# First MLP product: blocks 2 to 15 as seven half-size products, with the weight sums and the gate row moved

## The chip, the cores and the metric

The kernel runs on one core of one Trainium2 chip. The metric is device time in microseconds of one launch; lower is better. Each launch computes one layer for 512 frames of width 2048.

## The reference, cut to what matters

The change touches the second sub-layer and the adaLN gate of that sub-layer:

```python
mod = (c_act @ w_ada[i] + b_ada[i])          # six parts of 2048; the last is gate_f
h = rmsnorm(x, g_pre_mlp[i]) * (1.0 + scale_f) + shift_f       # (512, 2048)
y = jnp.square(jax.nn.relu(h @ w_mlp_in[i])) @ w_mlp_out[i]    # hidden width 8192
x = x + gate_f * rmsnorm(y, g_post_mlp[i])
```

"First MLP product" is h @ w_mlp_in, followed by the squared relu. Everything is float32.

## The kernel before

Every float32 operand of a matmul is split in two: a rounded high part (written by ScalarE, type float32r) and the low part, which is the operand less the high part (written by VectorE). A product is then three matmuls, high x high, high x low, low x high. `split_mm` (lines 847 to 851) issues them; lines 849, 850 and 851 are the three lines that the profile shows for TensorE.

The first MLP product runs over 16 blocks of 512 hidden features (FBS = 16). `mlp_in(b)` (line 1221) goes over 16 k-tiles and four tiles of 128 features, each `split_mm` with the weights as the stationary operand and 512 frames moving: 192 matmuls of 512 columns a block. Blocks alternate between two sets of four PSUM banks. Block 0 (`first_mlp_in`) is cut in pieces that follow the arrival of x.

Weights come in groups of four k-tiles, four groups (`MM_O`) a block, 1 MB each: SP's queue loads them (`load_m1`), ScalarE makes the high part (`split_hi_mlp`), VectorE the low part (`split_lo_mlp`), in two buffers. Each engine has its own program order, written out by hand, and semaphores couple them.

Behind a block, `hidden(b - 1)` runs on ScalarE (relu, square, high parts) and on VectorE, where four operations form the combinations (lines 2458 to 2464) that the second MLP product needs, since that product already works by seven half-size products for a pair of quarters; line 2469 makes their low parts. The finished hidden block (14 rows of 512 numbers a partition, 3.6 MB) goes to DRAM in two stores of 1.8 MB each (`store_hidden`), for blocks 0 to 13. Two hidden buffers alternate.

The gate row gate_f = c_act @ w_ada + b_ada is made in eight parts of 256 columns between the blocks: ScalarE scales one half of a loaded tile by c_act and GpSimd the other (`ada_times_c`, `ada_second`), VectorE sums over k (`ada_reduce`, line 1892), TensorE sums over partitions with a matrix of ones (`ada_rows`), VectorE adds the bias and multiplies by the gain (`gate_row`). GpSimd does nothing else in this stage. In the second MLP product it adds operands for the quarter sums (`b22_sums`, line 2764).

## Time and profile before

| | |
|---|---|
| time, median of 3 runs | 2184.85 us (2184.24 to 2184.99) |
| span of the profiled execution | 2183.1 us |
| TensorE busy | 2152.5 us, 99% of the span |
| VectorE, ScalarE, GpSimd busy | 1542.9, 892.7 and 356.4 us (71%, 41%, 16%) |
| DMA | 445.46 MB, mean 204 GB/s |

The page has no time of the profiled execution other than its span. The busy share of an engine is counted from its instructions; a matmul's record is longer than the distance to the next, so that distances between starts tell the rate. The first MLP product lies between about 871 and 1557 us, the second behind it.

### The profile page before, as it was taken

How to read it: one execution, taken by the hardware profiler on the slowest of the kernel's cores; microseconds unless marked ns; L12 is line 12 of the kernel's file. 1: busy time of each engine (PE TensorE's matmuls, PEld its weight loads, DVE VectorE, ACT ScalarE, POOL GpSimd, SP SyncE). 2: the span in 40 equal slices, each digit the busy share in tenths (PEclk: the TensorE clock that was granted, in tenths of full speed). 3: DMA queues.
4: the chain of work that ended last, by engine and by line, in shares of the span. 5: the costliest groups of instructions: out<-in, count | busy, mean ns of one | idle time of the engine just before them, and what ended most of it. 6: DMA issues, size and time to landing. Idle time of an engine off the chain costs nothing.

```text
span 2183.1 us, 26860 instructions
## 1 busy us (share of the span) xinstructions
PE 2152.5 (99%) x9807; PEld 1753.1 (80%) x9807; DVE 1542.9 (71%) x1618; ACT 892.7 (41%) x1197; POOL 356.4 (16%) x206
## 2 busy tenths in 40 slices
PE   6999999999999999999999999999999999999998
PEld 4688888777777888888888888888888888888886
DVE  7987667677887626744554365445789898898988
ACT  5353433342343325543533443435444444444443
POOL 1000000000000001000000000000036454453634
PEclk9999999999999999999999999999999999999999
DMA  9967657655554343665574665655374666567764
GB/s 361 355 223 229 211 159 249 199 174 167 152 149 154 135 174 141 221 207 189 207 249 164 207 233 206 207 190 181 117 269 147 238 214 200 172 241 238 246 219 167
DMA packets 259333, 445.46 MB, mean 204 GB/s; under 512 B 18380, under 2 KB 102672, under 8 KB 253592
## 3 DMA queue, kind: packets, MB, share of 16 engines
q1 hardware_dynamic: 258976, 443.91, 60.5%
q8 instruction: 71, 1.16, 0.2%
q14 instruction: 38, 0.31, 0.0%
q10 hardware_dynamic: 248, 0.08, 0.0%
HBM read 384.14 MB, written 59.79 MB: 203 GB/s over the span
## 4 chain that ended last, share of the span: by engine, by line
PE 93%; DVE 2%; DMA 1%; SPq 1%; ACT 1%; issue 1%; DVEq 1%; POOL 0%; POOLq 0%; ACTq 0%
PE pair L849 29%; PE pair L851 29%; PE pair L850 29%; DMA am_item<-in_w_ada 1%; PE pair L1068 1%; PE pair L952 1%; PE pair L926 1%; SPq L667 0%; PE pair L943 0%; DMA w_raw<-in_w_in 0%; PE pair L992 0%; PE pair L1146 0%; PE pair L1041 0%; DVE gg L1927 0%; DVE w_lo L1835 0%
## 5 line engine op out<-in xcount | busy, mean ns | idle before, releaser
L849 PE MATMUL pair<-in_hi,w_hi 128*128 128x512 f32 (+1 forms) x1728 | 689.0, 399 | 0.1
L851 PE MATMUL pair<-in_hi,w_lo 128*128 128x512 f32 (+1 forms) x1728 | 670.8, 388 | 0.0
L850 PE MATMUL pair<-in_lo,w_hi 128*128 128x512 f32 (+1 forms) x1728 | 669.8, 388 | 0.0
L849 PEld LDWEIGHTS pair<-in_hi,w_hi 128*128 128x128 f32 x1728 | 324.7, 188 | 69.5 <-issue 5.8
L851 PEld LDWEIGHTS pair<-in_hi,w_lo 128*128 128x128 f32 x1728 | 324.4, 188 | 68.4
L850 PEld LDWEIGHTS pair<-in_lo,w_hi 128*128 128x128 f32 x1728 | 325.0, 188 | 64.9 <-issue 1.9
L849 PE MATMUL pair<-v_op,hid_r 128*128 128x512 f32 x896 | 348.7, 389 | 0.3 <-issue 0.3
L851 PE MATMUL pair<-v_op,hid_r 128*128 128x512 f32 x896 | 348.6, 389 | 0.0
L850 PE MATMUL pair<-v_op,hid_r 128*128 128x512 f32 x896 | 348.6, 389 | 0.0
L1843 DVE TENSOR_TENSOR w_lo<-w_raw,w_hi 128x2048 fp32r<-128x2048 f32 x62 | 144.6, 2332 | 287.8 <-ACT w_hi L1324 287.8
L2499 DVE TENSOR_TENSOR v_op<-v_raw,v_op 128x1024 fp32r<-128x1024 f32 x192 | 295.5, 1560 | 64.8 <-ACT v_op L1802 63.7
L1802 ACT ACTIVATE v_op<-v_raw 128x1024 fp32r<-128x1024 f32 x192 | 203.3, 1061 | 286.2 <-PE pair L851 268.0
L1324 ACT ACTIVATE w_hi<-w_raw 128x2048 fp32r<-128x2048 f32 x63 | 120.5, 1913 | 234.2 <-PE pair L851 234.2
L2764 POOL TENSOR_TENSOR v_sum<-v_raw,v_raw 128x512 f32<-128x512 f32 x60 | 149.2, 2514 | 367.8 <-DVE v_raw L2514 367.8
L1835 DVE TENSOR_TENSOR w_lo<-w_raw,w_hi 128x1536 fp32r<-128x1536 f32 (+2 forms) x78 | 137.1, 1758 | 88.5 <-ACT w_hi L1315 88.0
L849 PEld LDWEIGHTS pair<-v_op,hid_r 128*128 128x128 f32 x896 | 168.2, 188 | 35.7 <-ACT v_op L1802 0.7
L851 PEld LDWEIGHTS pair<-v_op,hid_r 128*128 128x128 f32 x896 | 168.2, 188 | 35.0
L850 PEld LDWEIGHTS pair<-v_op,hid_r 128*128 128x128 f32 x896 | 168.2, 188 | 34.9
L1315 ACT ACTIVATE w_hi<-w_raw 128x1536 fp32r<-128x1536 f32 (+2 forms) x78 | 116.0, 1487 | 177.2 <-PE pair L851 165.2
L2773 POOL TENSOR_TENSOR v_raw<-v_raw,v_sum 128x512 f32<-128x512 f32 x60 | 135.3, 2286 | 18.4 <-DVE v_op L2499 18.4
L2685 POOL TENSOR_TENSOR ada<-ada,c_act 128x2048 f32<-128x2048 f32 x8 | 30.5, 3817 | 588.7 <-DMA ada<-in_w_ada 553.3
L2555 DVE TENSOR_TENSOR y_t<-pair,y_t 128x1024 f32<-128x1024 f32 x104 | 124.9, 1214 | 0.7 <-PE pair L851 0.7
(286 smaller groups left out, 2302.6 us busy)
## 6 DMA issues: line engine op xcount, KB each, us to landing
w_raw<-in_w_mlp_in SPq DMA_DIRECT2D x64, 1024.0 KB, 5.3
v_raw<-in_w_mlp_out SPq DMA_DIRECT2D x128, 512.0 KB, 5.1
hid_r<-hid_scratch SPq DMA_DIRECT2D x112, 512.0 KB, 6.4
hid_scratch<-hid_r SPq DMA_DIRECT2D x28, 1792.0 KB, 6.9
am_item<-in_w_ada SPq DMA_DIRECT2D x64, 512.0 KB, 8.3
...
```

What stands on the lines that cost most here:

```text
L849: pe.matmul(dst, a[0], b[0], start=start, stop=False, skip_group_check=onto)
L850: pe.matmul(dst, a[0], b[1], start=False, stop=False, skip_group_check=onto)
L851: return pe.matmul(dst, a[1], b[0], start=False, stop=stop, skip_group_check=onto)
L1315: act.activation(view(w_hi[n]), view(w_raw[n]), ACT.Copy).then_inc(hi_done, 1)
L1324: act.activation(m1_hi[m1_slot(j)][:, :], w_raw[j % 2][:, :], ACT.Copy).then_inc(hi_done, 1)
L1802: act.activation(v_op[i % 4][:, 0, :], raw_of(u, p)[:, h, :], ACT.Copy).then_inc(v_hi, 1)
L1835: dve.tensor_tensor(view(w_lo[n]), view(w_raw[n]), view(w_hi[n]).bitcast(F32), ALU.subtract)\
L1843: dve.tensor_tensor(m1_lo[m1_slot(j)][:, :], w_raw[j % 2][:, :], m1_hi[m1_slot(j)][:, :].bitcast(F32), ALU.subtract).then_inc(lo_done, 1)
L2499: dve.tensor_tensor(v_op[i % 4][:, 1, :], raw_of(u, p)[:, h, :], v_op[i % 4][:, 0, :].bitcast(F32), ALU.subtract).then_inc(v_lo, 1)
L2555: return dve.tensor_tensor(dst, src[:, :, :], dst, ALU.add)
L2764: last = pool.tensor_tensor(v_sum[:, h, cols], v_raw[q[B22]][:, h, cols], v_raw[q[B11]][:, h, cols], ALU.add)
L2773: last = pool.tensor_tensor(b21, b21, v_sum[:, h, cols], ALU.subtract)
```

## The change

Blocks 0 and 1 stay as they are. Each of blocks 2 to 15 is done in two half-blocks (`u` = 0 to 27; an even `u` is the first of its block). For the frames in two halves, the input features in two halves, and two groups of 128 hidden features of the block, the product is a 2 x 2 block product, and Winograd's form of Strassen's method makes it of seven products of half the size, in the order P1, P7, P6, P2, P5, P4, P3. Each is 8 `split_mm` with 256 columns. The sums of x that it needs (three tiles made new, one in place of a quarter of x) are made once, during block 1, by GpSimd and VectorE. The sums of weights are made for each half-block: the first, A21 + A22, on GpSimd (`sum_1`), three more on VectorE. Sums of results are made in PSUM: by accumulating onto a bank, by two copies on ScalarE, and by two additions on VectorE (`make_u3`, `make_c22`).

Weights come as quarters, 8 k-tiles x 128 columns, 512 KB in rows of 512 bytes, into five buffers; operands go through three buffers, one product each. There is one hidden buffer for blocks 0 to 14 in place of two, and relu and squares take 1024 elements at once. The gate row is made by 32 fused multiply-adds of 1024 columns on VectorE (`gf_step`) from whole rows of w_ada, with four sums over partitions on TensorE (`gf_rows`) and one multiplication by the gain each. The eight-part form of it, with its GpSimd and ScalarE work, is gone. Operand buffers of the second MLP product and the order of its PSUM pairs are renamed, and the last block's relus and squares go by quarters.

The diff, cut to its core:

```diff
-    M_END = M_MLP + FBS * MM_O
+    NB = 2
+    M_END = M_MLP + NB * MM_O
+    STEPS = 7
+    SUBS = 2 * (FBS - NB)
+    ALL_STEPS = STEPS * SUBS
...
+        A11, A21, A22, SUM, A12 = range(5)
+        SW_SLOT = ((0, 1, 2, 3, 4), (1, 0, 3, 2, 4))
+        SW_OPERAND = (A11, A21, A11, A12, SUM, A22, A12)
+        F_P1, F_P7, F_P6, F_P2, F_P5, F_P4, F_P3 = range(7)
+        C_X, C_Y, C_W, C_Z = range(4)
...
+            def load_quarter(u, role):
+                n = SW_SLOT[u % 2][role]
+                k = slice(0, XQ) if role in (A11, A21) else slice(XQ, KT)
+                col = block_of(u) * FBLK + (HALF if role in (A21, A22) else 0) + u % 2 * P
+                sp.dma_start(sw_raw[n][:, :, :], w_m1_t[:, k, col:col + P]).then_inc(sw_in[n], 16)
...
+            for u in range(SUBS):
+                b, following = block_of(u), u + 1 < SUBS
+                stored = u % 2 and b - 1 < FBS - 2
+                sp.wait_ge(sw_lo_done, step_end(u, F_P7))
+                if following:
+                    load_quarter(u + 1, A11)
+                else:
+                    sp.wait_ge(sw_used, step_end(u, F_P7))
+                    load_m2(0, B11)
+                    load_m2(0, B22)
+                if stored:
+                    store_hidden(b - 1, 0)
+                if following:
+                    sp.wait_ge(sw_lo_done, step_end(u, F_P6))
+                    sp.wait_ge(sw_sum, SW_SUM_0 + sums_of(u, S_4))
+                    load_quarter(u + 1, A21)
+                if stored:
+                    store_hidden(b - 1, 1)
+                if following:
+                    sp.wait_ge(sw_lo_done, step_end(u, F_P5))
+                    load_quarter(u + 1, A22)
+                    for g in GF_AT[u + 1]:
+                        load_gf(g)
+                    if u - 1 in GF_PART and GF_PART[u - 1] < 3:
+                        load_g_post(GF_PART[u - 1] + 1)
+                    sp.wait_ge(sw_lo_done, step_end(u, F_P3))
+                    load_quarter(u + 1, A12)
...
+            def strassen_in(u):
+                b, m = block_of(u), u % 2
+                for i in range(STEPS):
+                    n = STEPS * u + i
+                    pe.wait_ge(sw_hi_done, n + 1)
+                    pe.wait_ge(sw_lo_done, n + 1)
...
+                    if i == F_P7 and u - 1 in GF_PART:
+                        pe.wait_ge(gf_col, GF_COL_0 + GF_PART[u - 1] + 1)
+                    if i == F_P6:
+                        pe.wait_ge(p1_copied, u + 1)
+                    if i == F_P5:
+                        pe.wait_ge(u3_ready, u + 1)
+                    if i == F_P4 and u in GF_PART:
+                        gf_rows(u)
+                    if i == F_P3:
+                        pe.wait_ge(c22_ready, u + 1)
+                    dst = sub_bank(u, {F_P1: C_X, F_P2: C_X, F_P7: C_Z, F_P4: C_W}.get(i, C_Y))
+                    fresh = i in (F_P1, F_P7) and m == 0 or i == F_P7 and u == SUBS - 1
+                    for k in range(XQ):
+                        last = split_mm(dst, (sw_hi[n % 3][:, k, :], sw_lo[n % 3][:, k, :]), x_operand(i, k),
+                                        fresh and k == 0, k == XQ - 1, onto=True)
+                    last.then_inc(sw_used, 1)
...
+            def split_hi_step(n):
+                u, i = divmod(n, STEPS)
+                if i in (F_P1, F_P2, F_P4):
+                    done, count = sw_arrived(u, SW_OPERAND[i])
+                    act.wait_ge(done, count)
+                else:
+                    act.wait_ge(sw_sum, SW_SUM_0 + sums_of(u, {F_P7: S_3, F_P6: S_2, F_P5: S_1, F_P3: S_4}[i]))
...
+                else:
+                    act.wait_ge(sw_used, n - 2)
+                act.activation(sw_hi[n % 3][:, :, :], sw_tile(u, SW_OPERAND[i])[:, :, :], ACT.Copy).then_inc(sw_hi_done, 1)
...
+                for i in range(STEPS):
+                    if i == F_P2:
+                        copy_p1(u)
+                    if i == F_P5:
+                        copy_p7(u)
+                    split_hi_step(STEPS * u + i)
...
+                    if m == 0 and i in (F_P6, F_P2):
+                        relus(b - 1, i - F_P6)
+                    if m == 0 and i in (F_P5, F_P4):
+                        squares(b - 1, i - F_P5)
+                    if m == 0 and i == F_P3:
+                        hidden_hi(b - 1, 0)
+                    if m == 1 and i == F_P7:
+                        hidden_hi(b - 1, 1)
+                    if i == F_P6 and u in GF_PART:
+                        gf_high(GF_PART[u])
...
+            def x_sum(n):
+                dst, a, b, op = ((t1_raw, B12_HI, B11_HI, ALU.subtract), (t1_raw, t1_raw[:, :, :], t1_dif[:, :, :], ALU.add),
+                                 (t2_raw, B22_HI, t1_raw[:, :, :], ALU.subtract), (t2_raw, t2_raw[:, :, :], B22_LO, ALU.add),
+                                 (t4_raw, B21_HI, t2_raw[:, :, :], ALU.subtract), (t4_raw, t4_raw[:, :, :], B21_LO, ALU.add))[n]
+                if n == 0:
+                    dve.wait_ge(mod_lo, KT + N_PIECES)
+                    dve.wait_ge(x_tr, KT + N_PIECES)
+                if n == 1:
+                    dve.wait_ge(xs_pool, XS_POOL_0 + 4)
+                if n:
+                    dve.wait_ge(xs_raw, XS_RAW_0 + n)
+                dve.tensor_tensor(dst[:, :, :], a, b, op).then_inc(xs_raw, 1)
...
+            x_sum(0)
+            split_lo_mlp(MM_O)
+            x_sum(1)
+            x_sum(2)
+            split_lo_mlp(MM_O + 1)
+            combine(0, slice(0, SEQ), squares_to(0)).then_inc(h_comb, 1)
+            hidden_lo(0, 0)
+            x_sum(3)
+            split_lo_mlp(MM_O + 2)
+            hidden_lo(0, 1)
+            x_sum(4)
+            x_sum(5)
+            split_lo_mlp(MM_O + 3)
+            dve.memset(gg[:, :], 0.0).then_inc(gf_zero, 1)
+            x_low(0)
+            x_low(1)
+            def sum_3(u):
+                done, count = sw_arrived(u, A11)
+                dve.wait_ge(done, count)
+                dve.wait_ge(sw_sum, SW_SUM_0 + sums_of(u, S_1))
+                dve.tensor_tensor(sw_tile(u, A21)[:, :, :], sw_tile(u, A11)[:, :, :], sw_tile(u, A21)[:, :, :], ALU.subtract)\
+                    .then_inc(sw_sum, 1)
+            def sum_2(u):
+                dve.wait_ge(sw_lo_done, step_end(u, F_P1))
+                dve.wait_ge(sw_sum, SW_SUM_0 + sums_of(u, S_3))
+                dve.tensor_tensor(sw_tile(u, A11)[:, :, :], sw_tile(u, SUM)[:, :, :], sw_tile(u, A11)[:, :, :], ALU.subtract)\
+                    .then_inc(sw_sum, 1)
+            def sum_4(u):
+                dve.wait_ge(sw_lo_done, step_end(u, F_P2))
+                dve.wait_ge(sw_sum, SW_SUM_0 + sums_of(u, S_2))
+                dve.tensor_tensor(sw_tile(u, A12)[:, :, :], sw_tile(u, A12)[:, :, :], sw_tile(u, A11)[:, :, :], ALU.subtract)\
+                    .then_inc(sw_sum, 1)
+            def split_lo_step(n):
+                u, i = divmod(n, STEPS)
+                dve.wait_ge(sw_hi_done, n + 1)
...
+                    dve.wait_ge(sw_used, n - 2)
+                dve.tensor_tensor(sw_lo[n % 3][:, :, :], sw_tile(u, SW_OPERAND[i])[:, :, :],
+                                  sw_hi[n % 3][:, :, :].bitcast(F32), ALU.subtract).then_inc(sw_lo_done, 1)
+            def make_u3(u):
+                dve.wait_ge(sw_used, step_end(u, F_P6))
+                dve.wait_ge(p7_copied, u + 1)
+                dve.wait_ge(h_relu, relus_to(block_of(u) - 2))
+                dve.tensor_tensor(sub_bank(u, C_W), sub_bank(u, C_Y), p7_sb[:, :], ALU.add).then_inc(u3_ready, 1)
+            def make_c22(u):
+                dve.wait_ge(sw_used, step_end(u, F_P5))
+                dve.tensor_tensor(sub_bank(u, C_Z), sub_bank(u, C_Y), p7_sb[:, :], ALU.add).then_inc(c22_ready, 1)
+            def gf_step(g):
+                half, k = divmod(g, GF_ITEMS)
+                dve.wait_ge(gf_in[g % 2], GF_IN_0 + 16 * (g // 2 + 1))
...
+                    dve.wait_ge(gf_used, g)
+                part = gg[:, 1024 * half:1024 * half + 1024]
+                dve.scalar_tensor_tensor(part, gf_item[g % 2][:, :], c_act[:, k:k + 1], part, ALU.mult, ALU.add)\
...
+            def strassen_in(u):
+                b, m = block_of(u), u % 2
+                n0 = STEPS * u
+                if u == 0:
+                    sum_3(0)
+                split_lo_step(n0 + F_P1)
+                sum_2(u)
+                for g in GF_AT[u][:1]:
+                    gf_step(g)
+                if m == 1:
+                    hidden_lo(b - 1, 0)
+                split_lo_step(n0 + F_P7)
+                split_lo_step(n0 + F_P6)
+                if u == 0:
+                    x_low(2)
+                if m == 1:
+                    hidden_lo(b - 1, 1)
+                split_lo_step(n0 + F_P2)
+                sum_4(u)
+                if u == 0:
+                    x_low(3)
+                for g in GF_AT[u][1:]:
+                    gf_step(g)
+                split_lo_step(n0 + F_P5)
+                make_u3(u)
+                if u in GF_PART:
+                    gf_low(GF_PART[u])
+                split_lo_step(n0 + F_P4)
...
+                if m == 0:
+                    combine(b - 1, slice(0, SEQ), squares_to(b - 1)).then_inc(h_comb, 1)
+                split_lo_step(n0 + F_P3)
+                if u + 1 < SUBS:
+                    sum_3(u + 1)
+                make_c22(u)
+                if u in GF_PART:
+                    gf_columns(u)
...
-            with pool.Fori(0, FBS // 2) as g:
-                ada_second(g + Q_GF)
-            pool.wait_ge(ada_col, Q_GF + FBS // 2)
+            pool.wait_ge(w_used, M_MLP + 1)
+            pool.wait_ge(x_tr, KT + N_PIECES)
+            left, right = slice(0, HALF), slice(HALF, SEQ)
+            b12_lo = in_lo[:, 0:XQ, right].bitcast(F32)
+            pool.tensor_tensor(t3_raw[:, :, :], in_hi[:, XQ:KT, right].bitcast(F32), in_hi[:, 0:XQ, right].bitcast(F32),
+                               ALU.subtract).then_inc(xs_pool, 1)
+            pool.tensor_tensor(t3_dif[:, :, :], in_lo[:, XQ:KT, right].bitcast(F32), b12_lo, ALU.subtract).then_inc(xs_pool, 1)
+            pool.wait_ge(xs_pool, XS_POOL_0 + 2)
+            pool.tensor_tensor(t3_raw[:, :, :], t3_raw[:, :, :], t3_dif[:, :, :], ALU.add).then_inc(xs_pool, 1)
+            pool.tensor_tensor(t1_dif[:, :, :], b12_lo, in_lo[:, 0:XQ, left].bitcast(F32), ALU.subtract).then_inc(xs_pool, 1)
+            def sum_1(u):
+                for role in (A21, A22):
+                    done, count = sw_arrived(u, role)
+                    pool.wait_ge(done, count)
+                if u:
+                    pool.wait_ge(sw_lo_done, step_end(u - 1, F_P4))
+                pool.tensor_tensor(sw_tile(u, SUM)[:, :, :], sw_tile(u, A21)[:, :, :], sw_tile(u, A22)[:, :, :], ALU.add)\
+                    .then_inc(sw_sum, 1)
+            for u in range(SUBS):
+                sum_1(u)
```

## Rows read from the trace of the kernel before

**Rows 1.** Page, part 4: the chain that ended last, by engine.

```profile
PE 93%; DVE 2%; DMA 1%; SPq 1%; ACT 1%; issue 1%; DVEq 1%; POOL 0%; POOLq 0%; ACTq 0%
```

**Rows 2.** Stretches, first MLP product: busy us per engine, clock, DMA share, GB/s.

```profile
871.00:1571.00 700.00, 699.87 (x3137) 580.74 (x3137) 367.73 (x237) 293.28 (x370) 30.54 (x8) 1.00 0.60 202
```

**Rows 3.** ScalarE timeline (start us, duration us): first relu of blocks 0 and 5.

```profile
901.17 2.64 ACT L1705 ACTIVATE hid_f<-pair 128x512 f32<-128x512 f32 x4 [2.88 <-PE pair L851]
...
1119.99 2.58 ACT L1705 ACTIVATE hid_f<-pair 128x512 f32<-128x512 f32 x4 [7.17 <-PE pair L851]
```

**Rows 4.** TensorE timeline: two 256-column matmuls, nine starts apart.

```profile
850.47 0.28 PE L851 MATMUL pair<-in_hi,m_lo 128*128 128x256 f32 x1
...
851.54 0.28 PE L851 MATMUL pair<-in_hi,m_lo 128*128 128x256 f32 x1
```

**Rows 5.** VectorE timeline: prices and pitches of the operations that come up.

```profile
17.51 0.75 DVE L2113 SCALAR_TENSOR_TENSOR am_acc<-am_item,c_act,am_acc 128x512 f32<-128x512 f32 x1
18.17 0.75 DVE L2113 SCALAR_TENSOR_TENSOR am_odd<-am_item,c_act,am_odd 128x512 f32<-128x512 f32 x1
...
910.71 1.76 DVE L2469 TENSOR_TENSOR hid_r<-hid_f,hid_r 128x1536 fp32r<-128x1536 f32 x1
...
1117.27 0.42 DVE L1950 TENSOR_TENSOR gg<-pair,bg_bc 128x256 f32<-128x256 f32 x1 [2.12 <-PE pair L907]
...
1126.61 0.68 DVE L2458 SCALAR_TENSOR_TENSOR hid_f<-hid_f 128x512 f32<-128x512 f32 x1
...
1707.09 1.23 DVE L2499 TENSOR_TENSOR v_op<-v_raw,v_op 128x1024 fp32r<-128x1024 f32 x1 [1.50 <-ACT v_op L1802]
1708.23 2.35 DVE L2555 TENSOR_TENSOR y_t<-pair,y_t 128x1024 f32<-128x1024 f32 x2
1710.50 2.28 DVE L2514 TENSOR_TENSOR v_raw<-v_raw,v_raw 128x2048 f32<-128x2048 f32 x1
```

**Rows 6.** Timeline of GpSimd beside VectorE: who waits for whom.

```profile
1129.12 3.79 POOL L2685 TENSOR_TENSOR ada<-ada,c_act 128x2048 f32<-128x2048 f32 x1 [84.27 <-DMA ada<-in_w_ada]
1129.46 7.25 DVE L2469 TENSOR_TENSOR hid_r<-hid_f,hid_r 128x1536 fp32r<-128x1536 f32 x2
...
1712.91 2.15 POOL L2764 TENSOR_TENSOR v_sum<-v_raw,v_raw 128x512 f32<-128x512 f32 x1 [17.88 <-DVE v_raw L2514]
1713.83 2.32 DVE L2499 TENSOR_TENSOR v_op<-v_raw,v_op 128x1024 fp32r<-128x1024 f32 x1
```

**Rows 7.** Timeline of ScalarE: rounding a 1024-element operand.

```profile
1700.56 1.06 ACT L1802 ACTIVATE v_op<-v_raw 128x1024 fp32r<-128x1024 f32 x1 [1.66 <-PE pair L851]
```

**Rows 8.** DMA view: issues, KB each, median us to landing.

```profile
hid_scratch<-hid_r SPq DMA_DIRECT2D x28, 1792.0 KB, 6.9
ada<-in_w_ada SPq DMA_DIRECT2D x16, 1024.0 KB, 10.4
```

**Rows 9.** Timeline of SP's queue: issue of two loads with rows of 512 bytes.

```profile
1115.63 4.95 SPq L627 DMA_DIRECT2D ada<-in_w_ada  x2
```

**Rows 10.** Stretches: a load with 512-byte rows, and a hidden store, in transfer.

```profile
1123.00:1124.00 1.00, 1.00 (x6) 0.84 (x5) 0.00 (x0) 1.00 (x1) 0.00 (x0) 1.00 1.20 295
1139.00:1140.00 1.00, 1.00 (x6) 0.84 (x5) 0.00 (x0) 0.00 (x0) 0.00 (x0) 1.00 1.09 459
```

**Rows 11.** Timelines of GpSimd and VectorE at the end of block 0.

```profile
897.44 3.62 POOL L2685 TENSOR_TENSOR ada<-ada,c_act 128x2048 f32<-128x2048 f32 x1 [35.39 <-DVE in_lo L2376]
898.32 4.88 DVE L1843 TENSOR_TENSOR w_lo<-w_raw,w_hi 128x2048 fp32r<-128x2048 f32 x1 [1.12 <-ACT w_hi L1324]
```

**Rows 12.** TensorE's last group; stretches behind it (clock stands before DMA share).

```profile
2174.15 1.02 PE L1306 MATMUL pair<-y_t,v_sum 128*128 128x512 f32 x2
...
2175.00:2180.00 5.00, 0.17 (x1) 0.00 (x0) 4.33 (x5) 0.60 (x1) 0.00 (x0) 0.87 0.96 366
2180.00:2183.00 3.00, 0.00 (x0) 0.00 (x0) 0.00 (x0) 0.00 (x0) 0.00 (x0) 0.50 0.67 258
```

More of the change, by code:

```diff
@@ L272, in build_block @@
         w_in_s = [sem("w_in0"), sem("w_in1")]
-        ada_in = [sem(f"ada_in{u}") for u in range(2)]
         am_in = [sem(f"am_in{s}") for s in range(4)]
@@ new lines, in _ @@
+            store_hidden(0, 1)
+            sp.wait_ge(hi_done, M_END - 1)
+            sp.wait_ge(lo_done, M_END - 1)
+            load_quarter(0, A11)
+            load_quarter(0, A21)
+            sp.wait_ge(hi_done, M_END)
+            sp.wait_ge(lo_done, M_END)
+            load_quarter(0, A22)
+            sp.wait_ge(gf_zero, GF_ZERO_0 + 1)
+            sp.dma_start(gg[0:1, :], b_ada[0:1, GATE_F:GATE_F + D]).then_inc(gf_row, 16)
+            load_g_post(0)
+            sp.wait_ge(w_used, M_END)
@@ new lines, in hidden_hi @@
+            def hidden_hi(b, part):
+                hb = 1 if b == LAST else 0
+                act.wait_ge(h_sq, squares_to(b))
+                if part:
+                    act.wait_ge(h_comb, b + 1)
+                a, z = ((0, 3), (3, 7))[part]
+                act.activation(hid_r[hb][:, a:z, :], hid_f[hb][:, 7 + a:7 + z, :], ACT.Copy).then_inc(h_hi, 1)
+            for mm in range(MM_O):
+                if mm == 1:
+                    continue
+                split_hi_mlp(MM_O + mm)
+                if mm == 0:
+                    relus(0, 0)
+                    relus(0, 1)
+                    split_hi_mlp(MM_O + 1)
+                    squares(0, 0)
+                    squares(0, 1)
+                    hidden_hi(0, 0)
+                    hidden_hi(0, 1)
@@ new lines, in last_relu, with last_relu_one @@
+            def last_relu(first, half, done, count):
+                act.wait_ge(done, count)
+                cols = slice(half * HALF, half * HALF + HALF)
+                act.activation(hid_f[1][:, 6 + first:8 + first, cols], pair[2 * ((LAST + half) % 2) + first // 2][:, :, cols], ACT.Relu)\
+                    .then_inc(h_relu, 1)
+            def last_relu_one(n, done, count):
+                act.wait_ge(done, count)
+                act.activation(hid_f[1][:, 6 + n, RIGHT], bank[4 * (1 - LAST % 2) + n][:, RIGHT], ACT.Relu).then_inc(h_relu, 1)
@@ L1739, in raw_ready @@
+            for u in range(SUBS):
+                strassen_in(u)
             def raw_ready(u, p, h):
@@ L2479, in _ @@
[L2479 to L2493 removed]
+                    dve.wait_ge(sw_used, ALL_STEPS - 1)
@@ L2495, in split_operand, with hidden_end @@
+            for u in range(SUBS):
+                strassen_in(u)
+            def hidden_end():
+                combine(LAST, HIGH, squares_to(LAST)).then_inc(h_comb, 1)
+                hidden_lo(LAST, 0)
+                split_operand(3)
+                split_operand(4)
+                hidden_lo(LAST, 1)
+                split_operand(5)
+                seam_b12(0)
+                seam_sum(0)
             def split_operand(i):
```

469 lines of the change are left out of this document (282 added, 187 removed).

## The prediction

> **What bounds the kernel now.** I read the page first. TensorE is the chain: 93% of what ended last is its own work [rows 1], so time is gained only by fewer TensorE microseconds, and lost wherever TensorE is made to wait. Then the stretch view of the first MLP product: TensorE is busy 699.9 of 700 us, VectorE only 367.7 (53%), ScalarE 293.3, GpSimd 30.5, DMA engines 60% [rows 2]. The other engines have slack there on average; the change spends it. The relus of block 0 and of block 5 start 218.82 us apart, so a block takes 43.76 us [rows 3], 192 matmuls of 512 columns and a few small ones.
>
> **The gain.** A half-block (128 of the block's hidden features in each of the two halves, over all frames) becomes seven products of 8 x 3 matmuls of 256 columns. Nine starts of such matmuls with a weight load each lie 1.07 us apart, 0.119 us each [rows 4]. So a product is 24 x 0.119 = 2.85 us, a half-block 19.97, a block 39.95 against 43.76. Over 14 blocks that is -53.3 us if TensorE never waits. What remains is to see whether it waits. It does, at four places.
>
> **Prices.** VectorE, by pitch of successive operations [rows 5]: 1024 elements 1.15 us (1707.09 to 1708.23), 2048 elements 2.2, fused multiply-add with a column 0.66 for 512, so some 1.2 for 1024; 1536 elements 1.7; 256 elements from PSUM 0.42; the four combination steps of a hidden block 2.85 (1126.61 to 1129.46 in rows 6). ScalarE rounds 1024 elements in 1.06 [rows 7].
>
> GpSimd against VectorE is the price that matters. While GpSimd's 3.79 us operation ran, two VectorE operations worth 3.9 took 7.25: VectorE stood nearly as long as GpSimd worked. In the pair below, the VectorE operation that came while GpSimd had its turn took 2.32 for 1.2, and GpSimd's 512 elements took 2.15, of which the first 0.9 were a wait for VectorE's previous operation [rows 6]. They take turns by whole instructions when both read two operands in SBUF; GpSimd's own share is 1.1 us per 512 elements. So 1024 elements hold VectorE 2.2 us, 2048 hold it 4.4. The bounds are 0 (GpSimd's turn falls where VectorE waits anyway) and 2.2 per half-block; I take the full one where VectorE is late.
>
> The Trainium skill (GPSIMD Engine Reference, Engine selection) says that an elementwise sum of a tile belongs on VectorE and is about twice as slow on GpSimd. By it the first weight sum would cost VectorE 1.15 instead of 2.2; the rows' hold agrees in size, so here the move takes nothing off VectorE.
>
> **VectorE over one block.** 14 low parts and 6 sums x 1.15 = 23.0, four small ones 1.7, combination 2.85, low parts of the hidden block 3.9, 2.3 gate steps x 1.2 = 2.7, GpSimd's hold 2 x 2.2 = 4.4: 38.5 of 39.95 us. It was about 23. Nothing is left for its waits, and it waits in order: for P6 before `make_u3`, for the next half-block's GpSimd sum before `sum_3`, and `make_c22`, on which TensorE's last product P3 waits, stands behind `sum_3`.
>
> **First half of a block** (u even; zero is TensorE's start of P1; products end at 2.85, 5.7, 8.55, ...). P6 done 8.55, high part of P4 9.6, low part 10.8, combination of the previous block 13.65, low part of P3 14.8, `sum_3` 15.95, `make_c22` 16.4; GpSimd's sum falls into this (its A22 is asked for at 8.4 and is there at about 12) and holds it 2.2: 18.6. TensorE wants P3 at 17.1. Stall 1.5, half-block 21.5.
>
> **Second half** (u odd). VectorE enters 2.85 before zero and has two operations, a gate step, the first hidden low part (1.7) and P7's low part before TensorE's second product: 1.15 + 1.15 + 1.2 + 1.7 + 1.15 = 6.35, ready at 3.5 where 2.85 is wanted: stall 0.65. Then P6 4.65, second hidden low part 6.85, P2 8.0, `sum_4` 9.15 (A21 is asked for), P5 10.3 (A22 is asked for). SP's order puts both stores of the previous hidden block into the same queue ahead of A22. A store is 1.84 MB at 459 GB/s, 4.0 us; a quarter is 0.52 MB, 1.75 us at 295 [rows 10]. Issuing 2048 rows costs SP 2.5 us, a quarter's 1024 rows about 1.2 [rows 9]. A store lands 6.9 us after issue, of which 4.0 are transfer [rows 8]; I give a quarter 0.8 ahead and 0.9 behind. A11 is asked for at 3.5 and moves to 6.1; first store to 10.3; A21 12.1; second store 16.2; A22 18.1, landed 19.0. GpSimd's sum 21.2, `sum_3` 22.35, `make_c22` 22.8, against 17.8 wanted: stall 5.0. The half-block ends at 25.65. The bounds of this stall: 0.4 if A22 overtakes the store (landed 13.75, then VectorE's order alone: low part of P3 14.4, hold 16.6, `sum_3` 17.75, `make_c22` 18.2), 6 if the stores move at half the rate.
>
> A block is 21.5 + 25.65 = 47.15, with 0.1 for each of three restarts 47.45: +3.7 over 43.76. Blocks 2 to 14 have a store in their second half: 13 x 3.7 = +48. Block 15 has none, and no successor's sum: 21.5 + 20.6 = 42.1, -1.7.
>
> **The entrance** (block 1, where the sums of x are made). GpSimd and VectorE are released together at 897.4, behind the last low part of x [rows 11]. VectorE's first x difference 897.3 to 899.5; GpSimd's first of four 2048-element operations to 903.9; only then the low part of block 1's first weight group, 906.1. It ended at 903.2 before, just in time: stall 2.9. The next in VectorE's order, `x_sum(1)`, waits for all four of GpSimd: 910.5, 914.9, 919.3; two x sums 923.7, then the second group's low part 926.1. TensorE wants it at 906.2 + 10.9 = 917.1: stall 9.0. Later groups come in time. Together +12 (bounds 6 and 16: GpSimd's price per 2048 between the 3.6 of its broadcast multiply and 5). In the first half-block the low parts of x and the late loads of A22 and A12 put `make_c22` some 3.5 later than in the others: +3.5.
>
> **The rest.** The gate row loses 8 pairs of 256-column matmuls (8 x 0.24 = 1.9, contained in the 43.76 of a block) and has four pairs of 512 columns, 8 x 0.227 = +1.8. Its 32 multiply-adds are in VectorE's sum; eight 3.8 us GpSimd multiplies, sixteen VectorE reductions and ScalarE's scaling go, all of it hidden before, worth nothing. Loads of w_ada stay about the size they were and follow A22. ScalarE has per block 14 x 1.06 and 8 or so for the hidden block and copies, 23 of 40: hidden. The seam to the second product: last relus and squares by quarters on ScalarE, +1 (0 to 4). Renamed PSUM pairs and moved operand buffers cost nothing: the same number of banks, no order changed.
>
> **Sum**, on the profiled execution (span 2183.1): -53.3 is contained in the blocks; +48 - 1.7 + 12 + 3.5 + 1.8 + 1 = +64.6, a span of 2247.7. The page gives no time around the span; the median of the runs lies 1.75 above it, so 2249.5, rounded 2250.
>
> **Rivals.**
> 1. *The covers hold: faster.* GpSimd's turn falls into VectorE's waits, the stores don't delay A22, and TensorE runs through: -53.3 + 12 + 1.8 + 1 = -38.5, 2146. For it: VectorE was busy 53% [rows 2]. Against it: the sum of 38.5 in 39.95. It decides as soon as `make_c22` ends by 17.1 in both halves.
> 2. *The stores alone don't obstruct* (A22's packets slip in between). Second half 21.0, block 42.8, -1.0 x 13, with the entrance and the rest +4: 2189, between 2175 and 2205.
> 3. *The clock falls in the stalls.* Behind the last matmul group (ends about 2175.2) the granted clock is 0.87 on average over 2175 to 2180 and 0.50 after [rows 12]: full until about 2178.7, then 1.2 GHz. So idling 3.5 us brought it down once. A 5 us stall could; P3 at 1.2 GHz would take up to 24 x 0.107 = 2.6 more. 14 stalls x 0 to 2.6, say 2.3: +32, 2282. Against it: one observation, at the end of the program. The Trainium skill (TensorE: Matmul & The Clock Gate, HAM oscillation) describes this loss for a kernel that waits for a load between groups of matmuls.
> 4. *The change doesn't thin the columns' cost*: if a 256-column matmul cost 0.13 because three weight loads no longer hide, a block would be 43.7 without any stall. Rows 4 show 0.119 with the loads; the chance is small and it lies inside the slow cases.
>
> **Chances.** Forecast (2225 to 2268) 0.50; clock 0.18; stores out of the way 0.17, of which 0.09 slower, 0.04 the same, 0.04 faster; covers hold 0.15. Faster by over 0.2% (about what a measurement of this kernel can tell from no change) 0.19, within 0.2% 0.04, slower 0.77. The range goes from 2187 (into the second rival) to 2292 (the clock's full price); about 2 in 10 lie outside, nearly all on the fast side.
>
> **What would show it.** In the profile after: 256-column matmuls 0.119 apart within a product; TensorE idle ahead of P3, some 1.5 us in even and 5 in odd half-blocks, released by VectorE's `make_c22` addition; ahead of that `sum_3` waiting for GpSimd, and GpSimd for A22's DMA, whose landing takes 8 us or more in odd half-blocks and under 5 in even ones; VectorE over 80% busy in this stage; a stall of some 9 us at the second weight group of block 1; clock rows below 1.00 if rival 3 holds. If GpSimd's sum is done before VectorE reaches `sum_3`, or A22 lands early in the odd halves, the forecast is wrong on the side of the first two rivals.

## The result, and the profile after

The changed kernel takes 2320.74 us (median, 2318.82 to 2322.03) against 2184.76 for the kernel before: ratio 1.062, 95% interval [1.061, 1.064]. It is slower by 136 us, where +65 (2250, range 2187 to 2292) was forecast: the direction was right, the size half of what it is. The profiled spans are 2319.4 and 2183.1, 136.3 apart.

The page of the kernel after: busy times, the chain by engine, the two dearest groups of the new product, GpSimd's sum, and two kinds of DMA (last column: us from issue to landing).

```profile
PE 2156.3 (93%) x11815; PEld 1853.5 (80%) x11815; DVE 1745.4 (75%) x1903; ACT 968.7 (42%) x1222; POOL 423.0 (18%) x230
...
PE 68%; DMA 9%; DVE 9%; issue 6%; POOL 4%; ACT 2%; DVEq 1%; SPq 1%; POOLq 0%; ACTq 0%
...
L975 PE MATMUL pair<-in_hi,sw_hi 128*128 128x256 f32 x896 | 273.8, 306 | 117.7 <-DVE pair L2800 117.1
...
L3141 POOL TENSOR_TENSOR sw_raw<-sw_raw,sw_raw 128x1024 f32<-128x1024 f32 x28 | 74.6, 2663 | 672.0 <-DMA sw_raw<-in_w_mlp_in 672.0
...
sw_raw<-in_w_mlp_in SPq DMA_DIRECT2D x112, 512.0 KB, 4.9
...
hid_scratch<-hid_r SPq DMA_DIRECT2D x28, 1792.0 KB, 9.8
```

TensorE's own work was 93% of the chain [rows 1] and is 68% now. DMA, VectorE and GpSimd together are 22% of it, and the group of matmuls behind `make_c22` (L2800) stood 117.1 us. A hidden store lands 9.8 us after issue instead of 6.9 [rows 8].

The stretch view of the new product (busy us of TensorE, its weight loads, VectorE, ScalarE, GpSimd; then granted clock, DMA share, GB/s), beside [rows 2]:

```profile
1050.00:1500.00 450.00, 370.54 (x2862) 366.56 (x2862) 297.79 (x280) 194.86 (x207) 44.35 (x17) 0.91 0.53 179
```

TensorE is busy 82% instead of 100%, VectorE 66% though it is what TensorE waits for, and the clock is 0.91 on average. An engine busy for two thirds of a stage can hold the whole stage up if it waits in order. The waits of VectorE and GpSimd name whom it waits for (us in total, times, longest):

```profile
DVE sw_raw L2767 <- POOL sw_raw L3141: 142.9, 25, 9.9
...
DVE sw_lo L2789 <- ACT sw_hi L1928: 87.3, 69, 5.0
```

The first row is the stall's last link but one: `sum_3` waits for GpSimd's sum.

One odd half-block, followed back from the matmul that waited. First SP's queue, then GpSimd, VectorE and TensorE (start us, duration, in brackets the idle time before and its releaser):

```profile
1200.85 0.37 SPq L693 DMA_DIRECT2D sw_raw<-in_w_mlp_in  x1
1201.26 0.58 SPq L687 DMA_DIRECT2D hid_scratch<-hid_r  x1
1206.63 0.37 SPq L693 DMA_DIRECT2D sw_raw<-in_w_mlp_in  x1
1207.04 0.72 SPq L687 DMA_DIRECT2D hid_scratch<-hid_r  x1
1207.81 0.43 SPq L693 DMA_DIRECT2D sw_raw<-in_w_mlp_in  x1
1208.29 4.37 SPq L700 DMA_DIRECT2D gf_item<-in_w_ada  x1
```

```profile
1218.22 2.34 POOL L3141 TENSOR_TENSOR sw_raw<-sw_raw,sw_raw 128x1024 f32<-128x1024 f32 x1 [26.35 <-DMA sw_raw<-in_w_mlp_in]
```

```profile
1220.67 1.23 DVE L2767 TENSOR_TENSOR sw_raw<-sw_raw,sw_raw 128x1024 f32<-128x1024 f32 x1 [8.41 <-POOL sw_raw L3141]
1221.81 0.43 DVE L2800 TENSOR_TENSOR pair<-pair,p_sb 128x256 f32<-128x256 f32 x1
```

```profile
1222.38 0.55 PE L975 MATMUL pair<-in_hi,sw_hi 128*128 128x256 f32 x1 [6.79 <-DVE pair L2800]
1222.73 0.41 PE L976 MATMUL pair<-in_lo,sw_hi 128*128 128x256 f32 x1
1222.94 0.41 PE L977 MATMUL pair<-in_hi,sw_lo 128*128 128x256 f32 x1
...
1226.27 0.28 PE L977 MATMUL pair<-in_hi,sw_lo 128*128 128x256 f32 x1
1226.39 0.28 PE L975 MATMUL pair<-in_hi,sw_hi 128*128 128x256 f32 x1
```

A22, the quarter of weights that the sum waits for, is issued at 1207.81, behind two stores of 1.84 MB in the same queue. GpSimd gets to its sum at 1218.22, 10.4 us later, and passes it on at 1220.56. `sum_3` and `make_c22` follow, and TensorE has stood 6.79 us. `make_c22` itself reads neither A22 nor the sum; it only stands behind `sum_3`. When TensorE starts again its matmuls are 0.21 us apart, and 0.12 again from about 1225.7 on. The stretch view of that stall:

```profile
1219.00:1222.00 3.00, 0.00 (x0) 0.00 (x0) 1.33 (x2) 0.07 (x1) 1.56 (x1) 0.50 0.37 93
1222.00:1225.00 3.00, 2.62 (x12) 2.65 (x13) 2.97 (x4) 0.98 (x1) 0.00 (x0) 0.50 0.03 5
1225.00:1226.00 1.00, 1.00 (x8) 1.00 (x7) 1.00 (x2) 0.00 (x0) 0.00 (x0) 0.69 0.00 0
1226.00:1229.00 3.00, 3.00 (x27) 3.00 (x26) 1.85 (x2) 1.97 (x2) 0.00 (x0) 1.00 0.17 46
```

The granted clock is 0.50 (1.2 GHz) from 1219 on and stays there 3 us into the work. The Trainium skill (TensorE: Matmul & The Clock Gate, HAM oscillation) describes this loss: the clock falls while TensorE waits for a load, and the next products start slow. The rows agree with it.

**The 136 us by place.** The product starts at 962.2 instead of 946.9 (+15.3 in the entrance). Its 14 blocks end at 1693.1 instead of 1558.2, that is 730.9 us instead of 611.3 (+119.6). What follows is 1.4 longer. In the middle a block takes 52.63 us (twelve periods, from TensorE's restart at 1011.84 to that at 1643.38), where 47.45 was forecast. By the starts of the matmuls over these periods:

| us a block | forecast | measured |
|---|---|---|
| 336 matmuls and gate rows at full clock | 39.95 | 40.4 (0.1200 apart) |
| first matmuls after a pause | 0.3 | 0.3 |
| pauses between matmuls, pitch taken off | 7.15 | 9.45 |
| matmuls at the low clock, above their full-clock time | 0 | 2.4 |

The first row holds the gate row's matmuls too, which the forecast had in a term of its own (1.8 us over 14 blocks). The last row counts the intervals between 0.16 and 0.235 us, some 28 a block, less the 0.1 to 0.2 us a block which such intervals cost in the kernel that hardly waits (experiment `e11_p7_early` below).

### The profile page after: what moved, and what is told of

Same layout as the page of the kernel before. It is cut to its first block, busy times and chain, and to the rows that moved or that the text cites. A ratio compares the mean times of both kernels' runs of the same rounds, so it can differ in the third digit from the quotient of the medians.

```text
span 2319.4 us, 31846 instructions
## 1 busy us (share of the span) xinstructions
PE 2156.3 (93%) x11815; PEld 1853.5 (80%) x11815; DVE 1745.4 (75%) x1903; ACT 968.7 (42%) x1222; POOL 423.0 (18%) x230
## 4 chain that ended last, share of the span: by engine, by line
PE 68%; DMA 9%; DVE 9%; issue 6%; POOL 4%; ACT 2%; DVEq 1%; SPq 1%; POOLq 0%; ACTq 0%
PE pair L975 21%; PE pair L977 21%; PE pair L976 21%; DMA sw_raw<-in_w_mlp_in 9%; DVE sw_lo L2789 4%; POOL sw_raw L3141 3%; PE pair L1198 1%; PE pair L1082 1%; DVE gg L2810 1%; PE pair L1056 1%; DMA w_raw<-in_w_in 1%; DVE hid_r L2717 1%; ACT sw_hi L1928 1%; DVE sw_raw L2779 1%; PE pair L1073 0%
## 5 line engine op out<-in xcount | busy, mean ns | idle before, releaser
L975 PE MATMUL pair<-in_hi,sw_hi 128*128 128x256 f32 x896 | 273.8, 306 | 117.7 <-DVE pair L2800 117.1
L975 PE MATMUL pair<-in_hi,w_hi 128*128 128x512 f32 (+1 forms) x832 | 341.5, 410 | 12.5 <-DVE w_lo L2114 9.4
L1928 ACT ACTIVATE sw_hi<-sw_raw 128x1024 fp32r<-128x1024 f32 x196 | 207.5, 1059 | 343.1 <-PE pair L977 187.2
L977 PE MATMUL pair<-in_hi,w_lo 128*128 128x512 f32 (+1 forms) x832 | 323.1, 388 | 0.0
L976 PE MATMUL pair<-in_lo,w_hi 128*128 128x512 f32 (+1 forms) x832 | 322.1, 387 | 0.0
L2789 DVE TENSOR_TENSOR sw_lo<-sw_raw,sw_hi 128x1024 fp32r<-128x1024 f32 x196 | 244.9, 1255 | 88.2 <-ACT sw_hi L1928 87.3
L975 PEld LDWEIGHTS pair<-in_hi,sw_hi 128*128 128x128 f32 x896 | 189.8, 212 | 122.6 <-issue 121.8
L976 PE MATMUL pair<-in_lo,sw_hi 128*128 128x256 f32 x896 | 270.0, 301 | 0.0
L977 PE MATMUL pair<-in_hi,sw_lo 128*128 128x256 f32 x896 | 269.2, 300 | 0.0
L975 PEld LDWEIGHTS pair<-in_hi,w_hi 128*128 128x128 f32 x832 | 157.1, 189 | 47.9 <-issue 15.0
L975 PE MATMUL pair<-t_hi,sw_hi 128*128 128x256 f32 x672 | 190.6, 284 | 2.8 <-DVE sw_lo L2789 2.8
```

The costliest lines, as they stand in the source:

```text
L975: pe.matmul(dst, a[0], b[0], start=start, stop=False, skip_group_check=onto)
L976: pe.matmul(dst, a[0], b[1], start=False, stop=False, skip_group_check=onto)
L977: return pe.matmul(dst, a[1], b[0], start=False, stop=stop, skip_group_check=onto)
L1928: act.activation(sw_hi[n % 3][:, :, :], sw_tile(u, SW_OPERAND[i])[:, :, :], ACT.Copy).then_inc(sw_hi_done, 1)
L2789: dve.tensor_tensor(sw_lo[n % 3][:, :, :], sw_tile(u, SW_OPERAND[i])[:, :, :], sw_hi[n % 3][:, :, :].bitcast(F32), ALU.subtract).then_inc( ...
```

## The experiments

Ratios are to the kernel before (2184.7 to 2184.8 us). Theory: A22 lands late behind the stores; VectorE's fixed order hands that on to `make_c22` though it doesn't need it; every long stall also costs clock behind it. Rivals: VectorE or GpSimd is simply short of time; or the smaller matmuls are dear in themselves.

**`make_c22` ahead of `sum_3`** (`e1_c22_first`)

```diff
 split_lo_step(n0 + F_P3)
+make_c22(u)
 if u + 1 < SUBS:
     sum_3(u + 1)
-make_c22(u)
```

> Changed kernel with one edit: VectorE makes make_c22(u) before sum_3(u+1), so P3 no longer stands behind the chain A22 load, GpSimd sum, sum_3. Theory (order): the stall ahead of P3 goes in both halves (1.9 us in even, 6.9 in odd half-blocks of the trace after), but the low part of P1 of the next half-block still stands behind sum_3, one product (2.85 us) later, so the odd stall comes back there at about 4 us. Gain per block some 1.9 + 2.8 = 4.7 us, over 13 blocks some 60: about 2260. Rival (VectorE is simply full, 38.5 of 39.95 us counted): the stall only moves, total within 20 us of 2320.

Measured 2287.67 (2285.89 to 2290.40), ratio 1.047 [1.045, 1.049]: -33 where about -60 was expected. TensorE's waits:

```profile
PE pair L975 <- ACT sw_hi L1928: 64.5, 13, 6.3
PE pair L975 <- DVE sw_lo L2789: 25.5, 15, 2.2
```

The wait for `make_c22` is gone, but 13 waits of 5 us each (64.5 / 13) now stand at P1 of the next half-block. P1 needs no sum either: it reads A11, whose high part is long done, and its low part stands next behind `sum_3` on VectorE. The table names ScalarE's rounding, but the rounding that ends there is P7's, which waits for `sum_3`. The timeline of VectorE shows what P1 waited for: its low part ends at 1210.68, and TensorE starts at 1210.78:

```profile
1208.32 1.23 DVE L2767 TENSOR_TENSOR sw_raw<-sw_raw,sw_raw 128x1024 f32<-128x1024 f32 x1 [8.07 <-POOL sw_raw L3141]
1209.46 1.22 DVE L2789 TENSOR_TENSOR sw_lo<-sw_raw,sw_hi 128x1024 fp32r<-128x1024 f32 x1
```

So the late load is still there, and one reordering only moved the stall by a product.

**Stores behind A22** (`e2_stores_late`)

```diff
-if stored:
-    store_hidden(b - 1, 0)
 ...
-if stored:
-    store_hidden(b - 1, 1)
 if following:
     sp.wait_ge(sw_lo_done, step_end(u, F_P5))
     load_quarter(u + 1, A22)
+if stored:
+    store_hidden(b - 1, 0)
+    store_hidden(b - 1, 1)
```

> Changed kernel with one edit in SP's order: both stores of the hidden block are issued behind the load of A22 in place of ahead of it. Theory (queue): A22 lands some 5 us after its issue in odd half-blocks in place of 10.4, the stall there falls from 6.9 to some 1.5 us and the clock no longer drops there (it cost 1.4 us per stall): 13 x 6.5 = 85 us less, about 2235. Rival (latency of GpSimd and VectorE in the chain, not the queue): under 2 us a block, above 2295. What the delayed stores could cost: A12 and the gate rows land later; seen as a wait ahead of P2.

Measured 2258.49 (2256.91 to 2264.41), ratio 1.034 [1.033, 1.036]: -62 where 85 was expected.

```profile
PE pair L975 <- DVE pair L2800: 47.9, 27, 3.0
PE pair L975 <- DVE sw_lo L2789: 16.5, 19, 3.1
...
DVE gg L2810 <- DMA gf_item<-in_w_ada: 41.7, 12, 4.2
```

The wait for `make_c22` falls from 117.1 to 47.9; the stall in odd half-blocks is 1.9 us on average instead of 6.9. In exchange TensorE now waits 0.7 to 3.1 us ahead of P7 in most even half-blocks. The likely reason is that the gate rows' loads now lie behind the stores: VectorE waits 41.7 us for them in its order; this was not tested by itself. The experiment shows the queue: nothing but the place of two stores was changed. One stood ahead of A21 and both ahead of A22; now both stand behind these loads.

**The first weight sum on VectorE** (`e3_sum_on_vector`): the same addition, with the waits for its operands, at the head of `sum_3`; none on GpSimd.

```diff
-pool.tensor_tensor(sw_tile(u, SUM)[:, :, :], sw_tile(u, A21)[:, :, :], sw_tile(u, A22)[:, :, :], ALU.add)
+dve.tensor_tensor(sw_tile(u, SUM)[:, :, :], sw_tile(u, A21)[:, :, :], sw_tile(u, A22)[:, :, :], ALU.add)
```

> Changed kernel with the first of the four weight sums on VectorE (directly ahead of sum_3) in place of GpSimd. Theory (turns): GpSimd's 2.34 us is replaced by 1.15 in the chain ahead of P3 and holds VectorE no more: 1.2 us less per half-block, some 30 to 35 us in all, about 2288. Rival (VectorE is full and GpSimd relieves it): slower by 1.15 x 28 = up to 32 us, about 2350.

Measured 2292.75 (2289.83 to 2294.19), ratio 1.050 [1.048, 1.051]: -28, a little less than the 30 to 35 expected. TensorE's wait for `make_c22` is 90.1 us in 27 instead of 117.1.

**Another order in the entrance** (`e4_entrance`): both low parts of the first two weight groups ahead of the sums of x.

```diff
-x_sum(0)
 split_lo_mlp(MM_O)
-x_sum(1)
-x_sum(2)
 split_lo_mlp(MM_O + 1)
 combine(0, slice(0, SEQ), squares_to(0)).then_inc(h_comb, 1)
+x_sum(0)
 hidden_lo(0, 0)
 ...
```

> Changed kernel with VectorE's order in block 1 altered: the low parts of the first two weight groups come ahead of the sums of x. Theory: the stalls of 3.1 and 9.4 us at the first two weight groups go, and the low clock behind them (5 us off full in 900 to 950): 12 to 17 us less, about 2305. Rival (the sums of x then arrive too late for the first half-block): the stall moves behind block 1, less than 5 us gained.

Measured 2313.16 (2310.21 to 2320.33), ratio 1.060 [1.058, 1.062]: -7.6, where 12 to 17 was expected. Of the two entrance stalls (3.06 and 9.41) 1.0 and 4.5 are left, which the expectation took to go.

**Two orders together** (`e5_order_store`): `make_c22` and P1's low part ahead of `sum_3`, and the second store alone behind A22.

```diff
 if u == 0:
     sum_3(0)
-split_lo_step(n0 + F_P1)
+    split_lo_step(n0 + F_P1)
 ...
 split_lo_step(n0 + F_P3)
+make_c22(u)
 if u + 1 < SUBS:
+    split_lo_step(n0 + STEPS + F_P1)
     sum_3(u + 1)
-make_c22(u)
 ...
```

> Changed kernel with two edits: on VectorE make_c22(u) and then the low part of P1 of the next half-block ahead of sum_3(u+1); on SP the second store of the hidden block behind the load of A22 in place of ahead of it. Theory (order): with these, nothing that TensorE wants before P7 of the next half-block stands behind the load of A22 and GpSimd's sum, two products (5.7 us) more room than in the changed kernel; stalls of 9 us a block fall to under 1.5 and the clock stays up: a block about 41.5 us in place of 52.6, total about 2176. Rival (VectorE is full: 38.5 us of work counted in 39.95 us): a block stays at 44 us or more, above 2205, with TensorE waiting for low parts all over the half-block and not at one place.

Measured 2211.21 (2207.56 to 2213.96), ratio 1.013 [1.011, 1.014]: -109.5, against -145 expected. TensorE's wait for `make_c22` is 2.7 us, but it waits 26.2 us (16 times) for other low parts, all of them P7's, mostly 1.6 to 1.9 in odd half-blocks. The expectation took these as covered.

**With the entrance mended** (`e6_plus_entrance`): as the last, and in the entrance x sums 0 to 2 behind the third group's low part, the rest behind the fourth, and the low part of the second new x tile behind P1's.

> As e5_order_store, and VectorE's order in block 1 altered: low parts of the weight groups ahead of the sums of x, the low part of the second new x tile behind P1's. Theory: of the 3.1 and 9.4 us stalls some 3 to 5 us in all are left (low part of the third group, since GpSimd's four operations of 4.6 us hold VectorE in between): 8 to 12 us less than e5_order_store, about 2166. Rival: the sums of x arrive late for the first half-block, gain under 4.

Measured 2203.29 (2202.26 to 2204.02), ratio 1.008 [1.007, 1.010]: -7.9 by the edit, at the edge of what was expected.

**With the sum on VectorE** (`e7_plus_sum_on_vector`): as the last, with the edit of the third experiment.

> As e6_plus_entrance, with the first weight sum on VectorE in place of GpSimd. Theory (turns): GpSimd's 2.3 us hold is replaced by 1.15 us of VectorE's own work; where VectorE is close to the limit that is worth up to 1.15 us a half-block, 5 to 25 us less than e6. Rival (GpSimd's sum falls into VectorE's waits once the order is right): slower than e6 by up to 15.

Measured 2196.58 (2193.71 to 2199.25), ratio 1.005 [1.003, 1.007]: -6.7 by the edit, near the small end of what was expected.

**With the gate steps late** (`e8_plus_gate_late`): as the sixth, and the one or two gate steps of a half-block behind `make_u3`.

```diff
-for g in GF_AT[u][:1]:
-    gf_step(g)
 ...
-for g in GF_AT[u][1:]:
-    gf_step(g)
 split_lo_step(n0 + F_P5)
 make_u3(u)
+for g in GF_AT[u]:
+    gf_step(g)
```

> As e6_plus_entrance, with both gate multiply-adds of a half-block behind make_u3 in place of the first of them ahead of P7's low part. Theory: the 0.4 us wait ahead of P7 in odd half-blocks and any wait for the gate row's load go: 3 to 10 us less than e6. Rival: no change, as the multiply-adds only move to where make_c22 is due.

Measured 2184.15 (2182.35 to 2187.38), ratio 1.000 [0.999, 1.001]: -19 by the edit, two to six times what was expected. The first gate step stood ahead of P7's low part, for which the kernel of the fifth experiment waited.

**The clock by itself** (`e9_warm`): the changed kernel, and in its odd half-blocks TensorE multiplies a zero tile while it waits, which adds nothing to the result.

```diff
+zero_w = small("zero_w", [P, 32])
 ...
 if i == F_P3:
+    if m == 1 and u + 1 < SUBS:
+        for k in range(40):
+            pe.matmul(sub_bank(u, C_W)[0:32, :], zero_w[:, :].bitcast(F32R), t4_hi[:, k % XQ, :],
+                      start=False, stop=True, skip_group_check=True)
     pe.wait_ge(c22_ready, u + 1)
```

> The changed kernel with 40 matmuls of a zero weight tile (32 output columns, 256 moving ones, added onto a finished result, which they leave as it is) ahead of TensorE's wait for make_c22 in the 13 odd halves: TensorE works through about 4.8 us of the 6.9 us in which it stood. Theory: the idle stretch lets the clock fall, and in the changed kernel the matmuls behind the stall ran 0.213 us apart for 2.9 us (0.119 at the full clock), which costs 2.9 x (1 - 0.119/0.213) = 1.3 us a stall; without the fall 13 x 1.3 = 17 us go, to about 2304, and the granted clock of the stretch rises from 0.90 to 0.97 or more. Rival A: the clock costs more than that place shows (about 3 us a block are not accounted for by the stalls): about 2280. Rival B: the time behind the stall is set by VectorE's queue, which the clock does not touch, and a faster TensorE waits for it elsewhere: 2318 to 2321.

Measured 2302.29 (2298.12 to 2305.80), ratio 1.054 [1.052, 1.055]: -18.5 against -17 expected from the rows. No work was taken away; 520 matmuls came on top (13 x 40). It shows the clock's part, and not all of it:

```profile
1050.00:1500.00 450.00, 408.21 (x3276) 399.26 (x3276) 308.16 (x288) 200.52 (x212) 46.88 (x18) 0.97 0.53 181
...
1267.34 0.58 PE L976 MATMUL pair<-in_hi,sw_hi 128*128 128x256 f32 x1 [2.85 <-DVE pair L2805]
```

The clock is 0.97 instead of 0.91. It still falls where the zero products end before the wait does, as at 1267.34, where the first matmul behind 2.85 us of idleness takes 0.58 us instead of 0.36.

**Gate steps late, alone** (`e12_gate_late_alone`): the changed kernel with that one edit.

> The changed kernel with the one or two gate steps of a half behind make_u3, and nothing else. Theory: most gate steps stand ahead of weight steps with little slack, and in the kernel with the other orders mended this alone was worth 19 us; here the stalls at make_c22 are set by the landing of A22 and GpSimd's sum, so little of it is left: 2305 to 2318. Rival: the gate steps now stand nearer to sum_3 and make_c22 and push these later: 2322 to 2335.

Measured 2319.76 (2317.05 to 2321.21), ratio 1.062 [1.060, 1.063]: -1.0, which can't be told from nothing. The same edit was worth 19 us where the larger waits had gone.

**All of it** (`e10_sum_and_gate`) and **P7's low part early** (`e11_p7_early`): as the eighth with the sum on VectorE, then in addition:

```diff
+split_lo_step(n0 + F_P7)
 if m == 1:
     hidden_lo(b - 1, 0)
-split_lo_step(n0 + F_P7)
 split_lo_step(n0 + F_P6)
```

> All orders mended (make_c22 and P1's low part ahead of sum_3, the second store behind A22, the entrance, the gate steps behind make_u3) and the first weight sum on VectorE in place of GpSimd. Theory: the sum is no longer behind GpSimd's 2.34 us and its hand-over, worth 7 us in the kernel without the late gate steps; TensorE still waits 10.8 us for make_c22, of which half goes: about 2177 (2172 to 2182), below the kernel before. Rival: VectorE is busy 87% of the stretch already, and its 14 us more turn into waits for low parts: 2183 to 2192.

> As the kernel with the sum on VectorE and the gate steps late, and in addition P7's low part ahead of the first hidden low part in odd halves. Theory: TensorE's waits for a low part (10.2 us, 12 of them, in the kernel with the sum on GpSimd) are mostly those ahead of P7 in odd halves; they go, and the stores get their half a little later: 4 to 8 us less than the kernel without this edit, about 2170. Rival: the later hidden low part delays the first store and with it A21 and A22: the same or up to 5 us more.

Measured 2171.14 (2169.37 to 2172.64), ratio 0.994 [0.992, 0.995], and 2157.33 (2155.15 to 2158.44), ratio 0.987 [0.986, 0.989]: -13.0 by the sum (half of that was expected) and -13.8 by P7's low part (4 to 8 expected). TensorE's waits of the two in this product, and the stretch of the second:

```profile
PE pair L976 <- DVE sw_lo L2794: 13.1, 14, 1.7
...
PE pair L976 <- DVE sw_lo L2794: 1.3, 6, 0.5
...
1050.00:1500.00 450.00, 447.86 (x3707) 445.60 (x3707) 408.68 (x387) 251.39 (x269) 0.00 (x0) 1.00 0.67 226
```

The last kernel is the version that beats both: the change's arithmetic, with VectorE's and SP's orders made for it and one sum moved from GpSimd to VectorE, is 27.4 us (1.3%) faster than the kernel before. VectorE works 91% of the stretch, and TensorE hardly waits: it is busy 447.9 of 450 us. A block takes 41.0 us (1138.73 less 1015.62 is 123.1 for three).

## Why the prediction was wrong

*Right.* Each half-size matmul costs 0.120 with its weight load (forecast 0.119), so the fourth rival is out, and the gain is there: a block that hardly waits takes 41.0 us instead of 43.76. That is 2.8 a block where 3.8 was forecast (336 x 0.120 alone is 40.3; the gate row's matmuls and short pauses make up the rest). The place, the releaser and the order of the stalls were as forecast: in front of P3, long in odd and short in even half-blocks, released by `make_c22`, which stood behind `sum_3`, GpSimd and A22. The entrance was right to half a microsecond: stalls of 3.06 and 9.41 where 2.9 and 9.0 were forecast, because GpSimd's four operations ended at 904.28, 910.92, 915.59 and 920.10 where 903.9, 910.5, 914.9 and 919.3 were forecast. GpSimd's first two ran beside VectorE's operations and took 2.1 us longer than the last two, which ran alone:

```profile
897.58 6.70 POOL L3129 TENSOR_TENSOR t_raw<-in_hi 128x2048 f32<-128x2048 f32 x1 [35.22 <-DVE in_lo L2626]
904.24 6.68 POOL L3131 TENSOR_TENSOR t_dif<-in_lo 128x2048 f32<-128x2048 f32 x1
910.99 4.60 POOL L3133 TENSOR_TENSOR t_raw<-t_raw,t_dif 128x2048 f32<-128x2048 f32 x1
915.55 4.55 POOL L3134 TENSOR_TENSOR t_dif<-in_lo 128x2048 f32<-128x2048 f32 x1
...
899.75 6.68 DVE L2114 TENSOR_TENSOR w_lo<-w_raw,w_hi 128x2048 fp32r<-128x2048 f32 x1
920.13 2.29 DVE L2737 TENSOR_TENSOR t_raw<-t_raw,t_dif 128x2048 f32<-128x2048 f32 x1 [13.70 <-POOL t_dif L3134]
...
906.53 0.47 PE L975 MATMUL pair<-in_hi,w_hi 128*128 128x512 f32 x1 [3.06 <-ACT w_hi L1489]
927.10 0.77 PE L975 MATMUL pair<-in_hi,w_hi 128*128 128x512 f32 x1 [9.41 <-DVE w_lo L2114]
```

The first stall is put down to ScalarE, but VectorE's low part is what ends last there: 899.75 and 6.68 make 906.43.

*Wrong: the clock was left out of the sum.* The forecast took the stalls to leave the clock alone and gave the third rival, that it falls in them, 0.18. The rival was right: low-clock matmuls cost 2.4 us a block, 13 x 2.4 = 31, and about 2.2 more in the entrance, where eleven matmuls behind the 9.41 us stall were 0.43 apart instead of 0.23. That its price (+32) agrees with the sum is partly luck. It had 2.3 behind each long stall, with 0.107 for a matmul; the rows show 0.093 for a matmul and 1.9 behind each of the 13 long stalls, and the rest came behind shorter pauses, which it did not count. The zero products won 18.5 of it back by experiment. Of the 71.7 us that the forecast lacked, the clock made 33, the longer pauses 30 and the matmuls' own pace 6. The one row that spoke for it [rows 12], 3.5 us of idleness and then 0.50, was evidence enough for a 5 us stall; to call it one observation was the mistake. A shorter pause could do it as well, which that row had not shown. Behind one of 2.07 us the matmuls were 0.21 apart at once; behind the three of 1.50 they never were. Behind two of the seven pauses of 1.75 (up to 1299.24 and 1562.24) they started 0.12 apart and went over to 0.21 some 1.4 us later; the last two rows are the stretches of the first of these (TensorE's busy time, clock, DMA share, GB/s):

```profile
1194.58 0.36 PE L975 MATMUL pair<-in_hi,sw_hi 128*128 128x256 f32 x1 [1.50 <-DVE pair L2800]
1194.77 0.28 PE L976 MATMUL pair<-in_lo,sw_hi 128*128 128x256 f32 x1
...
1246.26 0.56 PE L975 MATMUL pair<-in_hi,sw_hi 128*128 128x256 f32 x1 [2.07 <-DVE pair L2800]
1246.61 0.42 PE L976 MATMUL pair<-in_lo,sw_hi 128*128 128x256 f32 x1
...
1299.00:1300.00 1.00, 0.76 (x6) 1.00 0.00 0
1301.00:1303.00 2.00, 2.00 (x11) 0.50 0.00 0
```

*Wrong in size: the odd stall.* Forecast 5.0, measured 6.9 (5.5 to 7.9 in the 13 of them). A22 was asked for 10.3 after the start of P1, as forecast, but the sum on GpSimd started 20.8 after it where 19.0 was forecast. The stores moved at about the rate used (444 GB/s for 459). It was the quarters that were priced too low. The sum had 295 GB/s for all of a quarter, but A11, issued at 1200.85, moved 74 and then 212 GB/s in its first two microseconds and its packets ran until about 1205, 7.5 after the start of P1 where 6.1 was forecast. A22 added some 0.4, and landed at 1218.10 (20.6 for 19.0). The end of `make_c22` came at 24.8 instead of 22.8. The stretches (TensorE's busy time, clock, DMA share, GB/s):

```profile
1202.00:1203.00 1.00, 1.00 (x11) 1.00 0.34 74
1203.00:1204.00 1.00, 1.00 (x10) 1.00 0.81 212
1204.00:1205.00 1.00, 1.00 (x11) 1.00 1.31 459
1206.00:1208.00 2.00, 2.00 (x19) 1.00 1.04 444
```

The forecast's mechanism is borne out by the store experiment. Its price for the stores in the odd half is 13 x (5.0 - 0.4) = 60 us; that run's -62 also holds clock won back and time lost to the late gate rows, so the agreement of the two figures is partly luck. SP's issue of a quarter took 0.37 us and not 1.2, which changed nothing here.

*Small.* The even stall was 1.84 instead of 1.5. The stall at P7 of odd half-blocks was 0.40, in about half of them, instead of 0.65 in all. The first half-block stood 3.5 us where 5.0 (1.5 and 3.5) was forecast. The seam and the gate rows came in as forecast: what follows the product is only 1.4 longer.

**The sum again.** A block is 5.18 over the forecast: pauses 2.3, clock 2.4, matmuls 0.45. Thirteen of them are 67; the entrance has 3.3 more (12 forecast, 15.3 measured, 2.2 of it clock). That is nearly all of the 71.7 us between +64.6 and +136.3.

*GpSimd's turn.* The forecast charged VectorE 2.2 us per half-block for it. With the sum on VectorE, 1.15 us is all that remains, and GpSimd's way lost 28, 6.7 and 13.0 us in the three pairs that differ only by it (two us, 0.5 and 1 a block). How much of this is the held VectorE and how much the longer way over GpSimd (2.34 us and two hand-overs in the chain behind A22) was not separated. VectorE's own load was forecast well: 38.5 less GpSimd's 4.4 and plus two sums is 36.4 us a block, and the last kernel shows 408.68 / 450 x 41.0 = 37.2. What the forecast didn't see is that this much fits: the rival "the covers hold" failed through the order, not through the load.
